# Two transformer blocks on one core: head norms and rotations moved into a projection, a shorter lag behind the gates, gates ahead of the residuals' roots, and a new order in S5

## The chip, the core and the metric

The kernel runs on one core of one Trainium2 chip, as one program with five instruction streams: PE (matmuls), DVE, ACT, POOL and SP, which here issues the DMAs. The metric is the device time of one execution in microseconds (us), median over runs.

## What is computed

512 tokens (256 of context, 256 latent) of width 1024 go through two blocks of two layers each, in float32. The parts that the change touches:

```python
def _rms(x, gain, eps=1e-6):
    xf = x.astype(jnp.float32)
    y = xf * lax.rsqrt(jnp.mean(xf * xf, axis=-1, keepdims=True) + eps)
    return (y * gain.astype(jnp.float32)).astype(x.dtype)
...
    gq, gk, gv, gog, gz, aq, ak, av = _split(h @ w_in, EVEN_SIZES)
    for d, z in enumerate(jnp.split(gz, 2, axis=-1)):
        logit = (z @ gla_w_gate[d] + gla_b_gate[d]).astype(jnp.float32)
        g = _heads(jax.nn.log_sigmoid(logit) / GLA_GATE_TAU, GLA_HEADS)
        dirs.append(_directional_scan(q, k, v, g, n_ctx, reverse=(d == 1)))
...
    qa = _rms(aq.reshape(B, N, ATT_KV_HEADS, ATT_GROUP, ATT_HEAD_DIM), att_q_norm).transpose(0, 2, 3, 1, 4)
    ka = _rms(ak.reshape(B, N, ATT_KV_HEADS, ATT_HEAD_DIM), att_k_norm).transpose(0, 2, 1, 3)
...
    q_lat = _rope(qa[:, :, :, n_ctx:], cos, sin)
    k_all = jnp.concatenate([ka[:, :, :n_ctx], _rope(ka[:, :, n_ctx:], cos, sin)], axis=2)
...
    x_lat = x_lat + m_lat[2] * _rms(o_lat @ w_out, norm_post_mix[l])
```

The first part is the norm; the next ones stand in the first mixer (a gated linear attention beside a softmax attention over k_all); the last line is the residual after a mixer, and the one after a feed-forward part is like it. `m_lat` and `m_ctx` are modulation vectors, products of the conditioning vector with mod_w. The S5 mixer of the second block is a diagonal complex state-space scan: inputs by `b_bar`, a scan over 128-token chunks, outputs by `c_mat`, for 64 groups and two directions.

## The kernel before

Activations stand feature-major: X and H are 128 partitions x 8 tiles x 512 tokens. A float32 product with a weight is made of three rounded ones: of every operand a rounded copy (ACT, `act_part`) and the rest (DVE, `dve_part`) are formed, in HP or XP for activations, in WP for weights. A weight "piece" is 128x1024; it is loaded by SP into one of four slots, split, and used by 24 matmuls.

Each engine has one hand-written order of instructions. `sig` marks an event, `wait_ge` waits for one, `fence` waits for a whole stage, and `take` and `until` hand out the eight PSUM banks. The stages are a list in `program`: the start (`First`), the first mixer (`Even`), feed-forward 0, the second mixer (`Odd`), feed-forward 1, the third mixer (`Mla`), MLP 0, `S5`, MLP 1.

`Even` has three parts. **The projection** (`Projections`, 50 to 166 us): shifts of h (`act_shift`, `dve_shift`), parts of h, then 20 pieces; pieces 12 to 15 give outputs by tokens (`tokens4_pe`), the last four by features (`four_pe`). Between pieces DVE builds the S5 and rotation tables two steps at a time (`beside`); SP stores them (`tables_sp`) and then fetches the mask msk, the gates' weights gla_gw and the constants cst. **The steps** (`Even.pe`, `act`, `dve`, `pool`; 22 of them, 168 to 379 us): step s works on attention unit s - LAG (16 units: scores, maxima, exponentials, transposes, values), on item s (a norm of 128 rows of heads, `RmsHeads`, and its rotation `Rope`, six of each), on the gates of the linear attention (`gates_*`, four of them), on its diagonal levels (`linear_*`), and on rows of the modulation product (`late_mods`: five groups of four steps, each with the two-slot loads of mod_w that `rows` uses, in slots 0 and 1). **The output projection** (`OutProj`, 379 to 423 us) takes its weights through the same slots; `EARLY` says which pieces and parts ACT and DVE prepare in the last three steps.

`Resid` follows the output projections and the feed-forward parts (even.res, ffn0.res over 512 tokens, odd.res, ffn1.res over 256). ACT squares the eight tiles, DVE adds pairs (`add_up`), PE sums over partitions, ACT forms the root as Ln and Exp, and then DVE does for each tile the multiplication with the root RS and, by halves, the addition into X with the factor CO. In ffn1.res PE also sums the squares of the context for the next mixer (`context_pe`), ahead of its own.

`S5` runs four turns u: PE transposes weights (`turn_pe`), ACT copies them to Wb (`turn_act`), PE forms inputs V (`inputs_pe`), DVE scans them (`scan_dve`), PE forms outputs.

In PE's steps late_mods sets which of the four groups of rows, q0 to q3, are read:

```python
            mods, r, k = self.late_mods(s)
            if mods:
                for q in ((0,), (1, 2), (3,), ())[k]:
```

Of the kernel before, what the change touches and what calls it, by code (L numbers as in the profile page):

```python
# [12 lines left out]
ALU = mybir.AluOpType  # L13
# [533 lines left out]
class Norm:  # L547
# [52 lines left out]
    def act(self, act, meanwhile=None):  # L600
        self.head_act(act, meanwhile)
        self.tail_act(act)

# [12 lines left out]

    def tail_act(self, act):
        p, n0 = self.p, self.n0
        self.mods.wait_co(act, self.j)
        for t in range(1, KT, 2):  # L620
            self.act_shift(act, t)
# [40 lines left out]
    def late_dve(self, dve):  # L662
        for t in range(0, KT, 2):
            self.dve_shift(dve, t)

    def parts_act(self, act):
        for k in range(KT):
            self.act_part(act, k)

# [4 lines left out]

    def parts_dve(self, dve):
        for k in range(KT):
            self.dve_part(dve, k)
# [34 lines left out]
class Resid:  # L712
# [3 lines left out]

    def __init__(self, p, name, down, src, n0, j, mods, sq):
# [3 lines left out]
        self.copied = 0 if down.banks is None and not down.add else None  # L721
        self.context = None

    def pe(self, pe):
        p, n, pe = self.p, T - self.n0, pe.on(self.name)
        banks = self.down.banks
        if banks is None:
            pe.core["free"][self.bank] = (self.name, ("y", 0))
# [7 lines left out]
        for t in range(KT):  # L736
            pe.until(t if banks is None else banks[t // 2], "y" if self.down.add else "yn", t)
        pe.until(self.bank, "lnsum")
        if self.context is not None:
            pe.core["free"][self.bank] = (self.context.stage, ("clnsum",))  # L740

    def act(self, act):
        p, n0, n, act = self.p, self.n0, T - self.n0, act.on(self.name)
        for t in range(KT):
            if self.down.add:
                act.wait_ge("y", t)
                y = self.down.Y[:, t, :]
            else:
                act.wait_ge("sum", self.down.c, t, of=self.src)
                y = self.down.at(t)  # L750
            act.act(self.sq[:, t, 0:n], y, ACT.Square).then_inc(*act.sig("sq", t))
# [4 lines left out]
        act.act(rs, rs, ACT.Exp, scale=-0.5).then_inc(*act.sig("rstd"))  # L756
        if self.context is not None:
# [10 lines left out]

    def dve(self, dve):
        p, n0, n, Y, dve = self.p, self.n0, T - self.n0, self.down.Y, dve.on(self.name)  # L770
        for t in range(KT):
            if self.down.add or t == self.copied:
                ps = dve.wait_ge("sum", self.down.c, t, of=self.src)[:, 0:n]
                if not self.down.add:
                    dve.wait_ge("sq", t)
# [3193 lines left out]
```

## Time and profile before

| | us |
|---|---|
| median of 3 runs | 2569.46 |
| lowest, highest | 2567.4, 2573.09 |
| the profiled execution | 2578.15 |
| its span in the trace | 2576.0 |

The span runs from the first to the last recorded instruction; what the execution takes beyond it is not in the trace. Starts are counted from the start of the span. A line of a timeline groups equal instructions that follow each other, with the time from the first one's start to the last one's end. L169, L200 and the like are lines of the helpers that issue matmuls and vector operations, so instructions are told apart by their tiles: sb_WP and sb_HP are the parts, sb_slot the slots, ps a PSUM bank. `PEclk` is the clock that was granted to PE, as a share of the full one.

### The profile page before, as it was taken

How to read it: one execution, taken by the hardware profiler on the slowest of the kernel's cores; microseconds unless marked ns; L12 is line 12 of the kernel's file. 1: busy time of each engine (PE TensorE's matmuls, PEld its weight loads, DVE VectorE, ACT ScalarE, POOL GpSimd, SP SyncE). 2: the span in 40 equal slices, each digit the busy share in tenths (PEclk: the TensorE clock that was granted, in tenths of full speed). 3: DMA queues.
4: the chain of work that ended last, by engine and by line, in shares of the span. 5: the costliest groups of instructions: out<-in, count | busy, mean ns of one | idle time of the engine just before them, and what ended most of it. 6: DMA issues, size and time to landing. Idle time of an engine off the chain costs nothing.

```text
span 2576.0 us, 35431 instructions
## 1 busy us (share of the span) xinstructions
PE 2343.0 (91%) x14834; PEld 1855.0 (72%) x14834; DVE 1501.4 (58%) x2352; ACT 1055.7 (41%) x1780; POOL 220.1 (9%) x302
## 2 busy tenths in 40 slices
PE   5987888999998988887999898989999999998999
PEld 2853455888875866666999672347878877878999
DVE  5337555656555487776544515555656564986554
ACT  3243444322233445554444425544332233335543
POOL 0001200000000033321000002110200200000110
PEclk8988989999999999999999999999999999999999
DMA  7135552444432455333654123342344424434453
GB/s 270 66 143 226 190 203 84 139 143 150 155 115 82 131 164 164 131 131 102 197 172 166 66 85 131 131 164 84 139 147 153 147 106 181 171 118 164 164 189 123
DMA packets 175279, 372.79 MB, mean 145 GB/s; under 512 B 8432, under 2 KB 101872, under 8 KB 160784
## 3 DMA queue, kind: packets, MB, share of 16 engines
q1 hardware_dynamic: 175120, 370.53, 41.0%
q8 instruction: 117, 1.92, 0.3%
q14 instruction: 42, 0.34, 0.0%
HBM read 340.07 MB, written 30.44 MB: 144 GB/s over the span
## 4 chain that ended last, share of the span: by engine, by line
PE 72%; DVE 13%; ACT 7%; issue 4%; DMA 3%; POOL 1%; SPq 0%; DVEq 0%; ACTq 0%; POOLq 0%
PE ps L169 71%; DVE sb_R L200 4%; ACT sb_R L252 2%; DVE sb_X L217 1%; DVE sb_WP L200 1%; DVE sb_H L200 1%; DMA sb_R<-mod_w 1%; DMA sb_slot<-mod_w 1%; DVE sb_cst L214 1%; ACT sb_R L258 1%; PE ps L179 1%; ACT sb_H L252 1%; DVE sb_cst L200 1%; DVE sb_R L232 1%; DVE sb_R L229 1%
## 5 line engine op out<-in xcount | busy, mean ns | idle before, releaser
L169 PE MATMUL ps<-sb_HP,sb_WP 128*128 128x512 f32 (+1 forms) x5736 | 1087.2, 350 | 39.7 <-DVE sb_HP L200 19.7
L169 PEld LDWEIGHTS ps<-sb_HP,sb_WP 128*128 128x128 f32 x5736 | 922.4, 192 | 188.0 <-DVE sb_HP L200 26.2
L200 DVE TENSOR_TENSOR sb_WP<-sb_slot,sb_WP 128x1024 fp32r<-128x1024 f32 x380 | 469.1, 1239 | 613.2 <-ACT sb_WP L258 612.8
L258 ACT ACTIVATE sb_WP<-sb_slot 128x1024 fp32r<-128x1024 f32 x380 | 399.1, 1056 | 745.6 <-PE ps L169 735.0
L169 PE MATMUL ps<-sb_XP,sb_WP 128*128 128x256 f32 (+1 forms) x2976 | 505.1, 333 | 15.3 <-DVE sb_XP L200 15.3
L169 PEld LDWEIGHTS ps<-sb_XP,sb_WP 128*128 128x128 f32 x2976 | 451.4, 193 | 69.0 <-DVE sb_XP L200 17.2
L200 POOL TENSOR_TENSOR sb_R<-sb_R 128x128 f32<-128x128 f32 (+2 forms) x194 | 155.3, 824 | 1581.7 <-ACT sb_R L252 1290.7
L200 DVE TENSOR_TENSOR sb_R<-sb_R 128x256 f32<-128x256 f32 (+3 forms) x398 | 201.1, 539 | 32.2 <-ACT sb_R L252 29.2
L169 PE MATMUL ps<-sb_R 128*32 128x64 f32 (+7 forms) x1768 | 162.6, 290 | 52.9 <-DVE sb_R L200 24.1
L169 PEld LDWEIGHTS ps<-sb_R 128*32 128x32 f32 (+4 forms) x1768 | 115.1, 155 | 109.0 <-issue 66.6
L252 ACT ACTIVATE sb_R<-ps 128x512 f32<-128x512 f32 (+1 forms) x208 | 99.7, 513 | 96.0 <-PE ps L169 92.5
L252 ACT ACTIVATE sb_R<-sb_R 128x512 f32<-128x512 f32 (+4 forms) x128 | 83.7, 663 | 121.5 <-DVE sb_R L200 119.9
L258 ACT ACTIVATE sb_R<-ps 128x512 f32<-128x512 f32 (+5 forms) x163 | 69.7, 495 | 109.5 <-PE ps L169 99.2
L169 PE MATMUL ps<-sb_H,sb_cst 128*128 128x256 f32 (+2 forms) x200 | 79.0, 542 | 33.1 <-ACT sb_H L252 29.2
L169 PE MATMUL ps<-sb_WP,sb_HP 128*128 128x512 f32 (+1 forms) x480 | 101.4, 371 | 4.5 <-DVE sb_HP L200 4.5
L169 PEld LDWEIGHTS ps<-sb_WP,sb_HP 128*128 128x128 f32 x480 | 85.5, 192 | 21.5 <-DVE sb_HP L200 5.3
L169 PEld LDWEIGHTS ps<-sb_H,sb_cst 128*128 128x128 f32 x200 | 37.8, 213 | 70.9 <-issue 29.5
L169 PE MATMUL ps<-sb_slot,sb_SX 128*2 128x512 f32 x544 | 72.6, 640 | 8.1 <-DMA sb_slot<-mod_w 8.1
L258 ACT ACTIVATE sb_slot<-ps 128x256 f32<-128x256 f32 (+3 forms) x124 | 45.5, 402 | 70.0 <-PE ps L179 43.3
L200 DVE TENSOR_TENSOR sb_cst<-sb_cst,sb_R 128x512 f32<-128x512 f32 (+1 forms) x112 | 72.2, 685 | 2.9 <-ACT sb_cst L252 2.5
L200 DVE TENSOR_TENSOR sb_XP<-sb_R,sb_XP 128x256 fp32r<-128x256 f32 (+1 forms) x116 | 64.8, 569 | 14.4 <-ACT sb_XP L258 13.9
L200 DVE TENSOR_TENSOR sb_R<-sb_slot,sb_R 128x2048 f32<-128x2048 f32 (+1 forms) x32 | 54.5, 1755 | 26.4 <-ACT sb_R L258 26.0
(142 smaller groups left out, 1822.8 us busy)
## 6 DMA issues: line engine op xcount, KB each, us to landing
sb_slot<-mlp_w SPq DMA_DIRECT2D x32, 2048.0 KB, 8.9
sb_slot<-mod_w SPq DMA_DIRECT2D x22, 2048.0 KB, 8.8
sb_R<-ada_w SPq DMA_DIRECT2D x12, 2048.0 KB, 7.4
sb_slot<-ada_w SPq DMA_DIRECT2D x24, 1024.0 KB, 4.8
sb_slot<-ffn_w_gate SPq DMA_DIRECT2D x22, 1024.0 KB, 5.3
sb_slot<-ffn_w_up SPq DMA_DIRECT2D x22, 1024.0 KB, 7.8
sb_slot<-ffn_w_down SPq DMA_DIRECT2D x10, 2048.0 KB, 7.7
sb_slot<-odd_w_in SPq DMA_DIRECT2D x32, 512.0 KB, 7.2
```

What stands on the lines that cost most here:

```text
L169: return self.e.matmul(out, w, x, start=start, stop=stop, skip_group_check=True)
L179: return self.e.transpose(out, a, self.p.c("ident"))
L200: return BLANK if self.e is None else self.e.tensor_tensor(out, a, b, op)
L214: return self.e.tensor_scalar(out, a, s1, None, op0) if op1 is None else self.e.tensor_scalar(out, a, s1, s2, op0, op1)
L217: return BLANK if self.e is None else self.e.scalar_tensor_tensor(out=out, in0=a, scalar=s, in1=b, op0=op0, op1=op1)
L229: return BLANK if self.e is None else self.e.reduce_max(out, a, AX.X)
L232: return BLANK if self.e is None else self.e.tensor_tensor_scan(out, a, b, 0.0, ALU.mult, op)
L252: return self.e.activation(out, a, func, bias=bias, scale=scale)
L258: return self.e.activation(out, a, ACT.Copy) if scale is None else self.e.activation(out, a, ACT.Copy, scale=scale)
```

## The change

It has six parts.

- Start of the projection: shifts, parts and the first three pieces are interleaved tile by tile (`FIRST`), where all shifts, then all parts, then the pieces stood.
- SP: two projection loads, then gla_gw and cst, then the rest of the projection; msk stays behind the tables.
- Items: norms and rotations are issued between projection pieces 12 to 19 (`ITEMS`, `between`), with banks 3 to 6 for the first ones; DVE's last rotation follows the projection.
- Steps: LAG is 2 for 4, so 20 steps. `late_mods` starts at step 0 for step 1, one step later relative to the units.
- `Resid`: the factor CO is multiplied before the root (`gate_act`, `gate_dve`; PSUM is free after it), blocks are two plain operations, tiles 2 and 5 on POOL. ffn1.res sums the context after its own sum.
- `S5`: turns go through i first and take banks 4 to 7 in the first turn; inputs wait for each half's Wb and each h; the scan starts after the first half of the inputs.

```diff
 class Resid:
+    POOL = (2, 5)
...
+        self.late = 6 if n0 == 0 else 8
...
         pe.vacant(self.bank)
-        if self.context is not None:
-            self.context.context_pe(pe, p.ps[self.bank])
         for g, group in enumerate(self.groups):
...
         pe.until(self.bank, "lnsum")
         if self.context is not None:
+            pe.vacant(self.bank)
+            self.context.context_pe(pe, p.ps[self.bank])
...
+    def gate_act(self, act, t):
...
+            i = act.copy(Y[:, t, a:b], y[:, a:b], self.mods.CO[:, self.j, w, t:t + 1])
+        i.then_inc(*act.sig("gated", t))
...
+    def block(self, e, t):
...
+        e.wait_ge("rstd")
+        e.wait_ge("gated", t)
+        e.mul(Y[:, t, :], Y[:, t, :], p.RS[:, n0:T]).then_inc(*e.sig("yn", t))
+        e.wait_ge("yn", t)
+        e.add(p.X[:, t, n0:T], p.X[:, t, n0:T], Y[:, t, :]).then_inc(*e.sig("x", t))
...
         for t in range(KT):
-            dve.mul(Y[:, t, :], y, p.RS[:, n0:T]).then_inc(*dve.sig("yn", t))
-            dve.wait_ge("yn", t)
-            for w, a, b in halves(n0):
-                i = dve.stt(p.X[:, t, a:b], Y[:, t, a - n0:b - n0], self.mods.CO[:, self.j, w, t:t + 1], p.X[:, t, a:b], ALU.mult, ALU.add)
+            if t not in self.POOL:
+                self.block(dve, t)
+    def pool(self, pool):
+        for t in self.POOL:
+            self.block(pool.on(self.name), t)
...
 class Projections:
+    FIRST = (0, 2, 4)
...
+            self.norm.dve_shift(e, 0)
+            self.norm.dve_shift(e, 2)
+            for t in range(KT):
+                if t in self.FIRST:
+                    self.pieces.dve_part(e, self.FIRST.index(t))
+                self.norm.dve_part(e, t)
+                if t % 2 == 0 and t + 4 < KT:
+                    self.norm.dve_shift(e, t + 4)
...
         for x in self.pieces.dve_ahead(e):
             next(beside, None)
             next(beside, None)
+            if between is not None:
+                between(x)
...
 class Even:
-    LAG = 4
+    LAG = 2
+    ITEMS = {12: (0, None), 13: (1, 0), 14: (2, 1), 16: (3, 2), 17: (4, 3), 18: (5, 4), 19: (None, 5)}
...
-        self.proj.sp(sp)
+        self.proj.first_sp(sp)
         e.fence(*self.before)
+        e.dma(self.gw[0:32], p.io["gla_gw"]).then_inc(*e.full("full_gw", "gw"))
+        e.dma(p.cst[:, 256:NEARLY], p.io["cst"][:, 256:NEARLY]).then_inc(*e.full("full_cst", "consts"))
+        self.proj.sp(sp, 2)
         self.params.tables_sp(sp)
-        e.dma(self.m, p.io["msk"]).then_inc(*e.full("full_late", "late_m"))
+        e.dma(self.m, p.io["msk"]).then_inc(*e.full("full_late", "late"))
...
-        r, k = divmod(s - 1, 4)
+        r, k = divmod(s, 4)
...
-    FIRST, VALUES = (4, 13), (12, 19)
+    FIRST, VALUES = (LAG, LAG + 9), (LAG + 8, LAG + 15)
     EARLY = ((0, 1), (0, 1)), ((2,), (2, 3)), ((), (4,))
...
 class S5:
-        for s in range(4):
-            if s == 3:
-                e.wait_ge("W3", u)
-            for i in range(2):
-                b, ps = e.take(0, 4)
+        for i in range(2):
+            for s in range(4):
+                if s == 3:
+                    e.wait_ge("W3", u)
+                b, ps = e.take(*(0, 4) if u else (4, 8))
...
-        e.wait_ge("Wb", u, 3, 1)
-        for k in range(KT):
-            e.wait_ge("h", k, of="s5.in")
         for i in range(2):
+            e.wait_ge("Wb", u, 3, i)
...
+                e.wait_ge("h", 4 * fh + f, of="s5.in")
...
-        e.wait_ge("V", u, 3, 1)
+        e.wait_ge("V", u, 3, 0)
...
         e.mul(T1, pr, Vr).then_inc(*e.sig())
+        e.mul(Vr, pi, Vr).then_inc(*e.sig())
+        e.wait_ge("V", u, 3, 1)
         e.mul(T2, pi, Vi).then_inc(*e.sig())
-        e.mul(Vr, pi, Vr).then_inc(*e.sig())
```

The first place in the order is PE at the end of the first mixer's projection, before. sb_WP,sb_HP are projection matmuls (pieces by tokens, then by features), `sb_R 128x512 x4` the gates' logits, `sb_cst 128x512` the sums of an item's norm, `sb_R,sb_cst 128x256` a rotation, `sb_slot0,sb_SX` rows of a modulation group from slot 0:

```order
L169 MATMUL ps<-sb_WP,sb_HP 128x512 x96
L169 MATMUL ps<-sb_HP,sb_WP 128x512 x96
L169 MATMUL ps<-sb_R 128x512 x4
L169 MATMUL ps<-sb_cst 128x512 x2
L169 MATMUL ps<-sb_R,sb_cst 128x256
L169 MATMUL ps<-sb_slot0,sb_SX 2x512 x8
L169 MATMUL ps<-sb_cst 128x512
L169 MATMUL ps<-sb_R,sb_cst 128x256
L169 MATMUL ps<-sb_slot1,sb_SX 2x512 x8
L169 MATMUL ps<-sb_slot0,sb_SX 2x512 x8
L169 MATMUL ps<-sb_cst 128x512
```

And now, from the first piece by features on:

```order
L169 MATMUL ps<-sb_HP,sb_WP 128x512 x24
L169 MATMUL ps<-sb_cst 128x512
L169 MATMUL ps<-sb_R,sb_cst 128x256
L169 MATMUL ps<-sb_HP,sb_WP 128x512 x24
L169 MATMUL ps<-sb_cst 128x512
L169 MATMUL ps<-sb_R,sb_cst 128x256
L169 MATMUL ps<-sb_HP,sb_WP 128x512 x24
L169 MATMUL ps<-sb_cst 128x512
L169 MATMUL ps<-sb_R,sb_cst 128x256
L169 MATMUL ps<-sb_HP,sb_WP 128x512 x24
L169 MATMUL ps<-sb_R,sb_cst 128x256
L169 MATMUL ps<-sb_R 128x512 x4
```

The items now stand between pieces of 24 matmuls, and the rows of the modulation follow the logits directly, with the first unit's scores (`sb_R 128x256 x2`) behind the third group of rows.

The second place is PE's last steps ahead of the output projection (`x192`), before. sb_slot2,sb_R are products of the linear attention, sb_cst,sb_slot3 transposes and sb_slot3,sb_R values of the attention:

```order
L169 MATMUL ps<-sb_slot2,sb_R 128x256 x2
L169 MATMUL ps<-sb_slot1,sb_SX 2x512 x8
L169 MATMUL ps<-sb_R,sb_cst 128x512 x2
L179 MATMUL ps<-sb_cst,sb_slot3 128x128 x4
L169 MATMUL ps<-sb_slot3,sb_R 64x128 x8
L179 MATMUL ps<-sb_cst,sb_slot3 128x128 x4
L169 MATMUL ps<-sb_cst,sb_RW 128x128 x4
L169 MATMUL ps<-sb_slot3,sb_R 64x128 x8
L169 MATMUL ps<-sb_HP,sb_WP 128x512 x192
```

And now:

```order
L169 MATMUL ps<-sb_slot2,sb_R 128x256 x2
L169 MATMUL ps<-sb_slot1,sb_SX 2x512 x8
L169 MATMUL ps<-sb_slot0,sb_SX 2x512 x8
L169 MATMUL ps<-sb_R,sb_cst 128x512 x2
L179 MATMUL ps<-sb_cst,sb_slot3 128x128 x4
L169 MATMUL ps<-sb_slot3,sb_R 64x128 x8
L179 MATMUL ps<-sb_cst,sb_slot3 128x128 x4
L169 MATMUL ps<-sb_slot1,sb_SX 2x512 x8
L169 MATMUL ps<-sb_slot3,sb_R 64x128 x8
L169 MATMUL ps<-sb_cst,sb_RW 128x128 x4
L169 MATMUL ps<-sb_HP,sb_WP 128x512 x192
```

Rows from slots 1 and 0 (q1, q2) now stand in the last unit's step, behind the linear attention, and the fourth rows behind the values of the next step; before, the fourth rows from slot 1 were the only ones there.

## Rows read from the trace of the kernel before

**Rows 1.** page, part 1: busy us, share of the span, instructions
```profile
PE 2343.0 (91%) x14834; PEld 1855.0 (72%) x14834; DVE 1501.4 (58%) x2352; ACT 1055.7 (41%) x1780; POOL 220.1 (9%) x302
```

**Rows 2.** page, part 4: shares of the chain that ended last
```profile
PE 72%; DVE 13%; ACT 7%; issue 4%; DMA 3%; POOL 1%; SPq 0%; DVEq 0%; ACTq 0%; POOLq 0%
```

**Rows 3.** windows: stretch, us, busy (instructions) by engine, PEclk, DMA share, GB/s
```profile
50.05:166.26 116.21, 116.21 (x552) 95.81 (x552) 43.46 (x114) 29.59 (x40) 0.00 (x0) 0.98 0.25 82
201.55:359.12 157.57, 121.09 (x951) 70.91 (x947) 105.33 (x188) 67.30 (x169) 30.27 (x18) 0.89 0.50 194
359.12:378.90 19.78, 17.46 (x109) 9.64 (x105) 6.35 (x8) 10.39 (x20) 0.00 (x0) 0.91 0.71 276
```

**Rows 4.** timeline 38 to 60, DVE and PE: start us, us, what, [idle before <-releaser]
```profile
48.69 4.62 DVE L200 TENSOR_TENSOR sb_WP<-sb_slot,sb_WP 128x1024 fp32r<-128x1024 f32 x4
...
50.05 20.17 PE L169 MATMUL ps<-sb_HP,sb_WP 128*128 128x512 f32 x80 [11.83 <-DVE sb_WP L200]
```

**Rows 5.** DMA issues from 21.8 to 22.1: KB each, median us to landing
```profile
sb_slot<-even_w_in SPq DMA_DIRECT2D x1, 2048.0 KB, 17.4
```

**Rows 6.** timeline, PE, 148 to 206
```profile
202.86 1.12 PE L169 MATMUL ps<-sb_cst 128*128 128x512 f32 x2 [0.60 <-ACT sb_cst L252]
```

**Rows 7.** timelines of DVE, SP and PE, 153 to 168; DMA issues at 158.9 and 160.2
```profile
153.53 0.06 DVE L223 MEMSET sb_RS<- 128x1 f32 x1
166.40 0.63 DVE L220 CAST sb_msk<-sb_R 128x896 uint8<-128x896 f32 x1 [12.81 <-DMA sb_cst<-cst]
...
158.98 0.33 SPq L263 DMA_DIRECT2D sb_R<-msk  x1
...
167.71 5.05 PE L169 MATMUL ps<-sb_R 32*128 32x512 f32 x8 [1.45 <-ACT sb_R L252]
...
sb_R<-msk SPq DMA_DIRECT2D x1, 448.0 KB, 2.9
...
sb_slot<-mod_w SPq DMA_DIRECT2D x1, 2048.0 KB, 11.0
```

**Rows 8.** timeline, PE: rows of two mod_w loads
```profile
193.59 3.49 PE L169 MATMUL ps<-sb_slot,sb_SX 128*2 128x512 f32 x16 [3.68 <-DMA sb_slot<-mod_w]
...
357.29 1.90 PE L169 MATMUL ps<-sb_slot,sb_SX 128*2 128x512 f32 x16 [0.35 <-DMA sb_slot<-mod_w]
```

**Rows 9.** DMA issues at 357.0 and 360.6; timeline, ACT, 346 to 382
```profile
sb_slot<-mod_w SPq DMA_DIRECT2D x1, 2048.0 KB, 7.3
...
sb_slot<-even_w_out SPq DMA_DIRECT2D x1, 512.0 KB, 8.8
...
372.27 2.00 ACT L258 ACTIVATE sb_WP<-sb_slot 128x1024 fp32r<-128x1024 f32 x2
```

**Rows 10.** timelines of DVE and POOL: a residual's block, POOL beside DVE
```profile
437.54 0.68 DVE L200 TENSOR_TENSOR sb_R<-ps,sb_RS 128x512 f32<-128x512 f32 x1
438.26 0.88 DVE L217 SCALAR_TENSOR_TENSOR sb_X<-sb_R,sb_CO,sb_X 128x256 f32<-128x256 f32 x2
...
207.95 2.96 DVE L200 TENSOR_TENSOR sb_R<-sb_R 128x512 f32<-128x512 f32 x3 [0.33 <-ACT sb_R L252]
...
208.09 1.67 POOL L200 TENSOR_TENSOR sb_R<-sb_R 128x512 f32<-128x512 f32 x1 [207.65 <-ACT sb_R L252]
211.05 2.51 POOL L200 TENSOR_TENSOR sb_R<-sb_R 128x512 f32<-128x512 f32 x2 [1.29 <-ACT sb_R L252]
```

**Rows 11.** timeline, PE, 1407 to 1428
```profile
1412.03 3.62 PE L169 MATMUL ps<-sb_H,sb_cst 128*128 128x256 f32 x16
```

**Rows 12.** timelines of PE and DVE in S5
```profile
2168.83 11.57 PE L169 MATMUL ps<-sb_H,sb_R 32*128 32x128 f32 x197 [2.49 <-ACT sb_H L252]
...
2289.74 6.69 DVE L200 TENSOR_TENSOR sb_R<-sb_slot,sb_R 128x2048 f32<-128x2048 f32 x3 [6.43 <-ACT sb_R L258]
...
2320.73 0.88 PE L169 MATMUL ps<-sb_R,sb_slot 128*32 128x64 f32 x48 [0.66 <-DVE sb_R L200]
```

More of the change, by code:

```diff
@@ L746, in act @@
                 act.wait_ge("y", t)
[L747 removed]
             else:
                 act.wait_ge("sum", self.down.c, t, of=self.src)
[L750 to L751 removed]
+            act.act(self.sq[:, t, 0:n], self.src_of(t), ACT.Square).then_inc(*act.sig("sq", t))
+        for t in range(4, self.late):
+            self.gate_act(act, t)
         act.wait_ge("sumsq")
@@ L756, in act @@
         act.act(rs, rs, ACT.Exp, scale=-0.5).then_inc(*act.sig("rstd"))
+        for t in range(self.late, KT):
+            self.gate_act(act, t)
         if self.context is not None:
@@ L891, in out_loads, with four_pe @@
     return [load(order[0:4]), load(order[4:8])]
-def four_pe(p, pe, pieces, x, n, u, cols):
+def four_pe(p, pe, pieces, x, n, u, cols, between=None):
     bs = []
@@ L942, in tokens4_pe @@
                 pe.E.at[pe.stage, "used", y] = pe.E.at[pe.stage, "out", u, 3]
+            if between is not None:
+                between(y)
 def narrow_pe(p, pe, pieces, u, blocks):
@@ L1324, in sp, with first_sp, pe @@
         self.pieces.sp(sp.on(self.name), None, first)
-    def pe(self, e):
+    def first_sp(self, sp):
+        for n in range(2):
+            self.pieces.load(sp.on(self.name), n)
+    def pe(self, e, between=None):
         p = self.p
@@ L1332, in pe @@
             if kind == "tokens":
-                tokens4_pe(p, e, pieces, u)
+                tokens4_pe(p, e, pieces, u, between)
             elif kind == "narrow":
@@ L1348, in act @@
             for _ in range(4):
-                next(ahead)
+                y = next(ahead)
+                if between is not None:
+                    between(y)
             for a, out in enumerate(outs):
@@ L1358, in act, with dve @@
                 i.then_inc(*e.sig("taken", u, a))
-    def dve(self, e, beside=()):
+    def dve(self, e, beside=(), between=None):
         if self.early:
-            self.norm.late_dve(e)
-            self.norm.parts_dve(e)
-            self.pieces.dve_first(e)
+            self.norm.dve_shift(e, 0)
+            self.norm.dve_shift(e, 2)
+            for t in range(KT):
+                if t in self.FIRST:
+                    self.pieces.dve_part(e, self.FIRST.index(t))
+                self.norm.dve_part(e, t)
+                if t % 2 == 0 and t + 4 < KT:
+                    self.norm.dve_shift(e, t + 4)
         else:
@@ L1370, in dve @@
             next(beside, None)
+            if between is not None:
+                between(x)
         for _ in beside:
```

150 lines of the change are left out of this document (81 added, 69 removed).

## Prediction

> **What bounds the kernel now.** I read the page first. PE is busy 91% of the span, DVE 58%, ACT 41% and POOL 9% [rows 1], and the chain that ended last runs 72% on PE, 13% on DVE, 7% on ACT and 3% on DMA [rows 2]. So an instruction costs what it weighs only where PE has no gap; elsewhere, moved work can be free. Then I cut the span at the stages and read busy time in each [rows 3]. The projection of the first mixer (50.05 to 166.26) has PE busy in all of its 116.21 us: work put there is paid in full. In the mixer's steps up to the last unit's scores (201.55 to 359.12) PE is busy for 121.09 of 157.57 us, at a clock of 0.89: these steps hang on hand-offs between engines and on the loads of mod_w as well as on PE. From the last scores to the output projection there are 19.78 us. Last I read single instructions at the places that the change touches.
>
> **Start of the projection.** DVE ends a piece by subtracting its rounded part, the first four from 48.69 on, and PE, which has stood idle for 11.83 us, begins at 50.05 [rows 4]. It needs only the first piece. The first load, issued at 21.89, lands 17.4 us later [rows 5], at 39.3. Now ACT copies piece 0 first (2.00 for two in rows 9, so 1.1 with its start, to 40.4), DVE subtracts it (4.62 / 4 = 1.16, to 41.6), then the first part, half as wide (0.6), so PE begins near 42.35: **-7.7**. Afterwards PE takes 5.5 us for a piece of 24 matmuls and the two other engines need about 2.7 for a part and a piece, so they stay ahead.
>
> **Norms and rotations in the projection.** Six matmuls of 128x512 and six of 128x256 come onto PE's full stretch. One matmul with float32 operands runs as two in the trace; a pair of the first kind took 1.12 with 0.60 of idle before it [rows 6], and the second is half as wide, 0.56. In a full stretch a wide matmul takes 116.21 / 552 = 0.21 for one split in three; at twice that for each half of a float32 one, 0.86 for a pair and 0.43 for a narrow pair, I get 6 x 0.86 + 6 x 0.43 = 7.7 at least, and 6 x 1.12 + 6 x 0.56 = 10.1 at most: **+8**, nearest to the row of full stretches, since the matmuls of the next piece fill what a pair would wait for. DVE and ACT are busy for 43.46 and 29.59 us of the 116.21 [rows 3], so their share of the items hides there. Sum of the two parts: the last projection matmul ends at about 166.7 instead of 166.3.
>
> **The mask arrives late.** DVE builds the rotation tables between pieces, 45 steps at two for a piece; the last five now stand behind the norm of item 5. They ended at 153.53 [rows 7]; I place them at 165.7. SP stores them, waits for the store, and issues msk 5.4 us after their end (158.98), which lands 2.9 later, and the cast of 0.63 follows. Before, that chain ended in cst (166.40), and PE's first logits began at 167.71. After: 165.7 + 5.4 + 2.9 + 0.64 = 174.6, and PE goes on at 175.0. The work that used to hide the mask is the projection itself; it no longer does. **+7.3** as a wait. The gates' weights and the constants, which SP now fetches before the projection's remaining loads, cost nothing: the projection moves 25% of what the DMA engines could [rows 3].
>
> **To the first scores.** The mod_w loads go out behind msk, at 171.4 instead of 160.30, and the third needs a slot that the first one's rows free. Before, PE read the third load's rows at 193.59 after waiting 3.68 us for it, and the first scores followed at 201.55 [rows 3, 8]. The first landed in 11.0 [rows 7]. After: rows of load one at 182 to 184, a load of 7.3 [rows 9] to 191.5, two us of rows, so scores at 193.4. With two steps fewer between the gates and the first unit this is **-8.2** against 201.55, everything above included.
>
> **The steps.** From first to last scores it was 157.57 us. Items are gone from units 0 to 3, but the gates of the second pair of heads now stand beside units 0 and 1, where they formerly ran ahead. I count **-2.5** (0 to -5 as bounds). The last unit's scores then start at 348.4.
>
> **The tail.** The output projection needs w_out in a slot, copied and subtracted. Before, the slot that its first load takes was free one step earlier: the last of that load's four parts was issued at 360.6 and took 8.8, and ACT copied at 372.27 [rows 9]. The first of the four was issued 1.3 earlier, so all have landed 10.1 after it. The mod_w schedule (late_mods) now stands one step later relative to the units, so rows q1 and q2 of the last group are read in the last unit's own step, as the second place in the order shows. They are read 12 to 16 us after its scores (an estimate: transposes, copies and values of two units stand before them in the order); then the load goes out and takes 10.1 for its parts; the two piece copies (2.00 in rows 9), their subtractions, the roots and the last turns take 11. That is 37 us from last scores to output projection, where 19.78 were needed: **+17**. Row 0 of the output projection would start at 385.4 instead of 378.90. A PE that has stood idle begins at less than its full clock (0.91 in the stretch before [rows 3]), about +0.8. Sum of all up to here: **+7.3**.
>
> **The four residuals.** In the two wide ones a block was 0.68 and 0.88 on DVE [rows 10], 1.515 with the overlap, eight of them 12.1. After: six blocks of two plain tensor operations, 1.33 each, 8.0. POOL takes blocks 2 and 5: four operations. POOL's 128x512 operation ran 1.67 beside DVE's three, which took 2.96 instead of 3 x 0.64 = 1.9 [rows 10]: about 1.0 lost to DVE for each. 8.0 + 4 x 1.0 = 12.0, and 12.7 if the ends don't meet: **+0.3** each. The gates before the root fit in the time in which PE sums squares. The odd residual, half as wide, likewise +0.3. In the last one (ffn1.res) 16 matmuls of the next mixer's context stood before the sums of squares, 3.62 us [rows 11]; they go behind the root. DVE's adds and ACT's squares bound it next, about 1.5 earlier only, and POOL gives back some of that: I take **-2.0**. Sum **-1.1**; bounds -4 (POOL free of cost) and +2. The Trainium skill (SBUF — State Buffer, section "SBUF: two separate sides") says that a GpSimd operation and a VectorE operation with two SBUF inputs exclude each other for the whole instruction. By that rule the 12 DVE operations and four POOL ones of a wide residual would follow each other, 12 x 0.68 + 4 x 1.26 = 13.2 with POOL's operation at 2.51 for two [rows 10], 1.1 more than now, and the four would sum to about +2.
>
> **S5.** PE's inputs began at 2168.83 after 2.49 us for the last shifted h; they now need the first of them only, and PE takes a second four banks for its turns, so that it starts these straight after its sum, ahead of a root step of about 0.9: together 3.4. Scan 3 starts its three multiplications (6.69) at 2289.74; two of them can now start ahead of the last input, worth up to 4.5, but PE waited only 0.66 for the scan's result at 2320.73 [rows 12], so little of that is seen before PE's own chain is earlier. So **-4.5**: 3.4 + 0.7 and about 0.4 between the two halves of the inputs; bounds -2 and -8.5.
>
> **Sum**: 7.3 - 1.1 - 4.5 = +1.7. On the profiled execution, 2578.15, this gives 2579.9. The median of the runs shown, 2569.46, is 8.7 below that execution; on it, 2571.2. I forecast **2571**. A difference under 0.2%, 5 us, is not told from none.
>
> **Rivals.** *The tail costs nothing* (0.30). w_out's slot may come free in time, or the units run closer together than before, since PE has 36 us idle in the 157.57 [rows 3]. For it: the wait in the tail is built from places in the order, not seen. Against: SP takes its loads strictly in turn. If the 17 us shrink to between 3 and 10, the time is 2557 to 2564: faster; I take 2561. *The mod_w loads fall behind at each group* (0.20). Loads go through slots that PE's rows free, and one takes 7.3 to 11.0 us [rows 7, 9] where a step takes about ten. With PE's rows one step later in the order and the units starting eight us earlier, two or three groups may each wait the 3.7 seen in rows 8: +9, that is 2580, slower. It decides from a step shorter than a load's landing. For it: the wait of rows 8 is there already. Against: the last group waited 0.35 [rows 8]. *POOL and DVE exclude each other* (0.08): the sum of the residuals is +2 instead of -1.1, the time 2574. For it: 2.96 for three operations that take 1.9. Against: only 1.0 was lost beside an operation of POOL that takes 1.26 alone. The Trainium skill's page SBUF — State Buffer is behind this one. My own case, with a wait for the mask and one for w_out, has 0.42, and its range by itself is 2565 to 2576.
>
> **Numbers.** The forecast is 2571. Faster by over 0.2% (under 2564.3): nearly all of the first rival and 0.02 of mine, 0.31. Slower (over 2574.6): the second rival, 0.03 of the third, 0.04 of mine, 0.27. The same: 0.42. The range leaves out the lowest and the highest tenth, which lie in the first two rivals: 2557 to 2582.
>
> **What would show it.** PE should begin the projection near 42.4 and the logits near 175; an idle time before the logits whose releaser is the cast of the mask is the third step. First scores near 193, last near 348, and a gap of PE before the output projection of over 10 us that ends with sb_WP or a load of w_out. In the residuals, DVE's operations longer than 0.69 beside POOL. In ffn1.res the root 2 to 3 us earlier. In S5 PE's inputs near 2166 in the old count. I am wrong if the output projection starts before 375 (tail), if the logits start at once after the projection (mask), or if the residuals change by more than 1 us each.

## The result

The changed kernel took 2589.11 us, median of 4 runs (2587.65 to 2590.69); the one before 2570.79 (2567.4 to 2573.09). The ratio is 1.0068, with a 95% interval of 1.0052 to 1.0084: some 18 us slower, outside the range of 2557 to 2582. The profiled execution of the changed kernel took 2590.69, its span is 2588.9.

The page of the changed kernel, parts 1 and 4, answers to [rows 1] and [rows 2]:

```profile
PE 2346.1 (91%) x14834; PEld 1863.1 (72%) x14834; DVE 1509.1 (58%) x2342; ACT 1063.9 (41%) x1804; POOL 240.4 (9%) x318
...
PE 74%; DVE 11%; ACT 7%; issue 4%; DMA 2%; POOL 1%; SPq 0%; DVEq 0%; ACTq 0%; POOLq 0%
```

PE's busy time rose by 3.1 us, the span by 12.9. So most of the loss is idle time of PE, and the page does not show where. The windows by stage do (the stretches of [rows 3], and between them the one from the projection to the first scores; the columns are the same):

```profile
41.23:172.95 131.72, 127.61 (x576) 102.51 (x576) 58.86 (x146) 48.81 (x73) 0.00 (x0) 0.95 0.17 55
172.95:202.87 29.92, 16.78 (x58) 3.90 (x57) 7.56 (x10) 9.98 (x15) 0.00 (x0) 0.61 0.83 333
202.87:358.17 155.30, 117.90 (x924) 69.75 (x920) 101.73 (x178) 64.99 (x165) 29.22 (x18) 0.87 0.49 191
358.17:396.54 38.37, 23.99 (x141) 11.70 (x137) 8.80 (x12) 14.68 (x26) 0.00 (x0) 0.78 0.48 181
```

The projection takes 131.72 us for 116.21, the steps 155.30 for 157.57, and the way from the last scores to the output projection 38.37 for 19.78. The granted clock fell where PE waits: 0.61 between projection and first scores, 0.78 in the tail. A share of 0.50 is the lower of the two levels, 1.2 GHz; the logits, behind PE's longest wait there, ran at 0.50 throughout (181.18 to 188.34). By landmarks, the change stands as follows on the kernel before (us, PE):

| landmark | before | forecast | after |
|---|---|---|---|
| projection starts | 50.05 | 42.35 | 41.23 |
| its last matmul ends | 166.3 | 166.7 | 172.9 |
| logits start | 167.71 | 175.0 | 181.18 |
| first scores | 201.55 | 193.4 | 202.87 |
| last unit's scores | 359.12 | 348.4 | 358.17 |
| output projection starts | 378.90 | 385.4 | 396.54 |
| next matmul behind even.res | 445.48 | | 464.31 |

PE's timeline of the changed kernel at the first four, against [rows 4], [rows 7] and [rows 8]:

```profile
41.23 48.41 PE L169 MATMUL ps<-sb_HP,sb_WP 128*128 128x512 f32 x201 [6.13 <-DVE sb_HP L200]
...
144.14 8.04 PE L169 MATMUL ps<-sb_HP,sb_WP 128*128 128x512 f32 x24 [4.11 <-DVE sb_cst L200]
...
181.18 7.16 PE L169 MATMUL ps<-sb_R 32*128 32x512 f32 x8 [8.23 <-DVE sb_msk L220]
...
199.34 3.60 PE L169 MATMUL ps<-sb_slot,sb_SX 128*2 128x512 f32 x16 [4.91 <-DMA sb_slot<-mod_w]
```

The start came as forecast. The wait of 4.11 us ahead of the piece at 144.14 was not in the forecast, and that piece took 8.04 us instead of 5.84, at a granted clock of 0.69 where the next piece had 1.00. DVE's timeline tells what released it:

```profile
141.64 1.23 DVE L200 TENSOR_TENSOR sb_WP<-sb_slot,sb_WP 128x1024 fp32r<-128x1024 f32 x1 [5.50 <-ACT sb_WP L258]
...
143.58 0.42 DVE L200 TENSOR_TENSOR sb_cst<-ps,sb_cst 128x256 f32<-128x256 f32 x1
```

The first matmuls of the pieces by features need a PSUM bank that holds item 1's rotated product. DVE reads it at 143.58, in the callback of piece 16, and that stands behind the subtraction of the next piece (141.64), which waits until ACT has copied the outputs by tokens. The bank is free 0.42 later, and PE goes on at 144.14. That this is the cause is a reading of the trace so far; e1_bank below tests it.

SP and the mask, against [rows 7]:

```profile
171.69 0.34 SPq L263 DMA_DIRECT2D s_tabc<-sb_R  x1
...
176.91 0.33 SPq L263 DMA_DIRECT2D sb_R<-msk  x1
177.29 195.28 SPq L263 DMA_DIRECT2D sb_slot<-mod_w  x20
```

The tables end at 171.67, behind the norm of item 5 as forecast, though 6 us later. msk goes out 5.2 later, is cast at 180.35, and the logits start at 181.18. In the tail, ACT, SP and PE, against [rows 9] and the second order:

```profile
358.31 14.26 SPq L263 DMA_DIRECT2D sb_slot<-mod_w  x2
373.92 21.41 SPq L263 DMA_DIRECT2D sb_slot<-even_w_out  x8
```

```profile
385.30 2.00 ACT L258 ACTIVATE sb_WP<-sb_slot 128x1024 fp32r<-128x1024 f32 x2 [13.86 <-DMA sb_slot<-even_w_out]
387.21 1.13 ACT L258 ACTIVATE sb_HP<-sb_H 128x512 fp32r<-128x512 f32 x2
388.25 0.57 ACT L258 ACTIVATE sb_slot<-ps 128x512 f32<-128x512 f32 x1
```

```profile
370.25 3.62 PE L169 MATMUL ps<-sb_slot,sb_SX 128*2 128x512 f32 x32
...
388.88 1.11 PE L179 MATMUL ps<-sb_cst,sb_slot 128*128 128x128 f32 x4 [11.64 <-ACT sb_slot L258]
...
396.54 3.70 PE L169 MATMUL ps<-sb_HP,sb_WP 128*128 128x512 f32 x15
```

SP issues the first part of w_out at 373.92, when PE has read the rows of slot 0 (the 32 matmuls from 370.25). ACT copies it at 385.30, and behind this copy stands the one that the last transposes wait for (388.25), so PE waits 11.64 us ahead of 388.88. That is the tail that the prediction priced at 37 us; it took 38.4.

A wide residual, even.res: DVE, POOL and PE, against [rows 10]:

```profile
444.44 0.69 DVE L200 TENSOR_TENSOR sb_R<-sb_R,sb_RS 128x512 f32<-128x512 f32 x1 [0.31 <-ACT sb_RS L252]
445.17 1.64 DVE L200 TENSOR_TENSOR sb_X<-sb_X,sb_R 128x512 f32<-128x512 f32 x1
446.73 1.75 DVE L200 TENSOR_TENSOR sb_R<-sb_R,sb_RS 128x512 f32<-128x512 f32 x1
448.51 1.64 DVE L200 TENSOR_TENSOR sb_X<-sb_X,sb_R 128x512 f32<-128x512 f32 x1
...
451.86 0.69 DVE L200 TENSOR_TENSOR sb_X<-sb_X,sb_R 128x512 f32<-128x512 f32 x1
```

```profile
444.49 1.77 POOL L200 TENSOR_TENSOR sb_R<-sb_R,sb_RS 128x512 f32<-128x512 f32 x1 [98.03 <-ACT sb_RS L252]
446.33 1.59 POOL L200 TENSOR_TENSOR sb_X<-sb_X,sb_R 128x512 f32<-128x512 f32 x1
447.89 1.71 POOL L200 TENSOR_TENSOR sb_R<-sb_R,sb_RS 128x512 f32<-128x512 f32 x1
449.68 1.60 POOL L200 TENSOR_TENSOR sb_X<-sb_X,sb_R 128x512 f32<-128x512 f32 x1
```

```profile
441.07 1.96 PE L169 MATMUL ps<-sb_H,sb_cst 128*128 128x512 f32 x4 [0.71 <-DVE sb_H L200]
447.61 2.05 PE L169 MATMUL ps<-sb_H,sb_cst 128*128 128x512 f32 x2 [4.59 <-ACT sb_H L252]
450.87 8.95 PE L169 MATMUL ps<-sb_H,sb_cst 128*128 128x512 f32 x14 [1.21 <-ACT sb_H L252]
464.31 6.05 PE L169 MATMUL ps<-sb_HP,sb_WP 128*128 128x512 f32 x14 [4.50 <-DVE sb_HP L200]
```

Beside POOL a DVE operation takes 1.64 to 1.75, alone 0.69. All six blocks take 12.1 us, as the eight did before. From PE's first sums to the next stage's first matmul it is 23.24 us instead of 21.98. PE sums the squares in the order of the tiles. Three of the four slowed operations stand in DVE's order ahead of the end of tile 1, at 450.15, and PE can go on with that tile only at 450.87; POOL's tile 2 had been ready since 447.92. From there the squares come bunched, and PE runs 14 matmuls from 450.87 to 459.82, 0.64 each, where it once kept up with tiles that came 1.52 apart. In ffn1.res PE now sums first:

```profile
1435.69 1.10 PE L169 MATMUL ps<-sb_R,sb_cst 128*128 128x256 f32 x4 [1.02 <-DVE sb_R L200]
1437.36 3.72 PE L169 MATMUL ps<-sb_H,sb_cst 128*128 128x256 f32 x16 [0.56 <-ACT sb_RS L252]
1442.49 3.69 PE L169 MATMUL ps<-sb_H,sb_cst 128*128 128x256 f32 x16 [1.41 <-ACT sb_H L252]
1450.26 6.28 PE L169 MATMUL ps<-sb_HP,sb_WP 128*128 128x512 f32 x14 [4.08 <-DVE sb_HP L200]
```

From the last projection matmul (1434.7) to the next stage's first (1450.26) it is 15.6 us; before it was 17.9, from 1412.2 to 1430.08, with the context's 3.62 us [rows 11] ahead of the sums. In S5, against [rows 12], the inputs start without a wait, straight behind the turns, and the scan begins with two multiplications ahead of the third:

```profile
2183.79 14.98 PE L169 MATMUL ps<-sb_H,sb_R 32*128 32x128 f32 x256
```

```profile
2298.16 4.49 DVE L200 TENSOR_TENSOR sb_R<-sb_slot,sb_R 128x2048 f32<-128x2048 f32 x2 [3.98 <-ACT sb_R L258]
2305.62 2.29 DVE L200 TENSOR_TENSOR sb_R<-sb_slot,sb_R 128x2048 f32<-128x2048 f32 x1 [2.97 <-ACT sb_R L258]
```

From the first sum ahead of S5 to the first matmul of MLP 1 it is 171.3 us (2171.73 to 2343.01) instead of 176.8 (2153.09 to 2329.90).

### The profile page after: what moved, and what is told of

Its sections match the earlier page's. It is cut to its first block, busy times and chain, and to the rows that moved or that the text cites. A ratio compares the mean times of both kernels' runs of the same rounds, so it can differ in the third digit from the quotient of the medians.

```text
span 2588.9 us, 35481 instructions
## 1 busy us (share of the span) xinstructions
PE 2346.1 (91%) x14834; PEld 1863.1 (72%) x14834; DVE 1509.1 (58%) x2342; ACT 1063.9 (41%) x1804; POOL 240.4 (9%) x318
## 4 chain that ended last, share of the span: by engine, by line
PE 74%; DVE 11%; ACT 7%; issue 4%; DMA 2%; POOL 1%; SPq 0%; DVEq 0%; ACTq 0%; POOLq 0%
PE ps L169 74%; DVE sb_R L200 3%; ACT sb_R L252 2%; DVE sb_WP L200 1%; DVE sb_H L200 1%; DMA sb_slot<-mod_w 1%; DVE sb_cst L214 1%; PE ps L179 1%; ACT sb_R L258 1%; DVE sb_cst L200 1%; ACT L245 1%; DMA sb_slot<-even_w_in 1%; DVE sb_X L217 1%; DVE sb_R L229 1%; ACT sb_H L252 1%
## 5 line engine op out<-in xcount | busy, mean ns | idle before, releaser
L169 PE MATMUL ps<-sb_R 128*32 128x64 f32 (+7 forms) x1768 | 166.3, 295 | 60.3 <-DVE sb_R L200 23.4
L169 PEld LDWEIGHTS ps<-sb_WP,sb_HP 128*128 128x128 f32 x480 | 85.5, 192 | 22.1 <-DVE sb_HP L200 5.3
L169 PE MATMUL ps<-sb_slot,sb_SX 128*2 128x512 f32 x544 | 76.2, 674 | 10.7 <-DMA sb_slot<-mod_w 10.7
```

Of the source, the lines that this page charges most:

```text
L169: return self.e.matmul(out, w, x, start=start, stop=stop, skip_group_check=True)
```

## The experiments

All ratios are to the kernel before, with 95% intervals; the changed kernel's is 1.0068. One thousandth is 2.6 us.

**The three waits, one by one.**

```diff
# e1_bank: items_dve
+        if y == 15:
+            self.rope_dve(dve, 1)
         if n1 is not None:
             dve.wait_ge("consts", of="even.in")
-            if n1:
+            if n1 not in (0, 2):
                 self.rope_dve(dve, n1 - 1)
```

> The changed kernel, but DVE's rotation of item 1 stands at projection piece 15 instead of 16, ahead of the preparation of the next piece. Theory A (PE's gap of 4.11 us ahead of the first piece by features is a wait for the PSUM bank that this rotation reads): the gap goes, and with it the slow clock behind it (8.04 instead of 5.84 us for that piece), 6.3 us in all; the tables, the mask, the logits and the first scores come 6 us earlier, and the time is near 2583. Rival B (the first scores are set by the mod_w loads, which do not care): the projection ends 6 us earlier and the first scores come at most 1 us earlier; the time stays near 2589.

Measured: 1.0052 (1.0037 to 1.0067), 4 us less than the change. PE at the first piece by features:

```profile
142.90 3.74 PE L169 MATMUL ps<-sb_HP,sb_WP 128*128 128x512 f32 x15 [0.69 <-ACT sb_cst L252]
```

The gap shrank from 4.11 to 0.69 us and the logits came at 175.23 instead of 181.18, the whole 6 us, and first scores at 197.06 for 202.87; the output projection started at 392.33, 4.2 earlier. The bank was the cause, and the loads did not hide it.

```diff
# e2_tables: Projections.dve
-            next(beside, None)
-            next(beside, None)
+            for _ in range(3):
+                next(beside, None)
```

> The changed kernel, but DVE makes three table steps per projection piece instead of two, so that they end at piece 15 instead of behind the last norm. Theory A: the mask is there before the projection ends; PE's wait of 8.23 us ahead of the logits goes, the logits run at the full clock, and the mod_w loads, which stand behind the mask on SP, go out as soon as their slots are free, so that the waits of 4.91 and 1.58 us for them shrink too. First scores 12 to 17 us earlier, time near 2575. Rival B (loads cannot start before the projection's last slots are free, about when the mask passes now): only 2 to 4 us.

Measured: 1.0027 (1.0013 to 1.004). PE at the end of the projection:

```profile
143.72 5.72 PE L169 MATMUL ps<-sb_HP,sb_WP 128*128 128x512 f32 x24 [3.32 <-DVE sb_cst L200]
...
172.28 6.82 PE L169 MATMUL ps<-sb_R 32*128 32x512 f32 x8 [2.07 <-DVE sb_R L200]
...
190.41 3.21 PE L169 MATMUL ps<-sb_slot,sb_SX 128*2 128x512 f32 x16 [5.89 <-DMA sb_slot<-mod_w]
```

The logits wait 2.07 us for DVE's last rotation and no longer 8.23 for the mask, and start 8.9 us earlier; the output projection started 13.5 earlier. But the logits kept the lower clock (6.82), and the third mod_w load was still awaited for 5.89, though the first two were issued from 143 on: its slot comes free only when PE reads the first rows. The first scores gained 9.3, not the 12 to 17 expected, so rival B was half right.

```diff
# e3_phase: late_mods and the groups of rows in PE's steps
-        r, k = divmod(s, 4)
+        r, k = divmod(s + 1, 4)
...
-                for q in ((0,), (1, 2), (3,), ())[k]:
+                for q in ((0,), (0, 1, 2) if s == 0 else (1, 2), (3,), ())[k]:
...
-        self.more.cols_dve(dve, 2)
```

> The changed kernel, but each modulation step is one step earlier relative to the attention units, as before the change: the first step reads three groups of rows, and the last group's third rows are read in the step before the last unit's. Theory A (the slot of w_out's first load comes free too late): PE's way from the last unit's scores to the output projection falls from 38.4 to about 20 us; the first scores may come up to 6 us later, since the fourth rows stand before them; time 2572 to 2578. Rival B (ACT's and DVE's preparation of w_out simply moved behind other work): the tail keeps over 30 us, time 2589 or more.

Measured: 1.0026 (1.0015 to 1.0036). The tail fell to 19.77 us:

```profile
369.30 1.13 PE L169 MATMUL ps<-sb_R 64*128 64x512 f32 x4
...
389.07 3.24 PE L169 MATMUL ps<-sb_HP,sb_WP 128*128 128x512 f32 x13
```

The first scores came 4.3 us later and the steps took 162.1 us, so in the profiled execution (2586.62 us, 5 above the median of its runs) the output projection started only 7.5 earlier; the ratio gives 11. The cause of the tail is shown: w_out's slot, through the place of the third rows. e4_three has all three edits.

> The changed kernel with all three edits of this batch: rotation 1 read earlier, three table steps per piece, modulation one step earlier. Theory A: the gains add up, 6 + 14 + 14, and the time is near 2555, faster than the kernel before by 0.6%. Rival B (one wait stands behind the other): the sum is no better than the best of the three alone by more than 5 us, so 2568 or more.

Measured: 0.9992 (0.9981 to 1.0003), 19 us less than the change, near to the sum of the single gains (4 + 11 + 11 = 26 at most) but with some of it hidden. So the three waits together cost about as much as the change lost. Yet 2555 was not reached, although start and S5 should gain some 13 us (7.7 and 5.4): theory A's sum fell short, and where these gains went is taken up with e13 below.

**The residuals and S5.** e5_resid_only and e6_s5_only put one class of the change's diff into the kernel before, `Resid` with its calls on POOL, and `S5`.

> The kernel before with only the residuals of the change (gates ahead of the root, plain blocks, tiles 2 and 5 on POOL, the context behind the root in ffn1.res). Prediction: the four residuals together -1.1 us, 2570 on the old median. Theory C (the squares come in another order and bunched, so that PE's sums behind them run late and slowly): the three others 1 to 1.5 us longer each from the root to the next matmul, ffn1.res 1 to 2 shorter; +2 in all. Rival D (DVE and POOL exclude each other for the whole time): wide residuals +1.2 in DVE's own blocks already.

> The kernel before with only the new order in S5. Predicted -4.5 us; in the changed kernel the stage took 4.5 less. Theory: it is worth the same alone, since nothing in it hangs on the other parts: ratio 0.998. Rival: part of it was the loads and the state of the clock that the stage was entered with, and alone it gives under 2 us.

Measured: the residuals 1.0014 (1.0003 to 1.0024), so 3.6 us slower; S5 0.9979 (0.9968 to 0.9991), 5.4 faster. From PE's sums to the next stage even.res took 23.20 instead of 21.98, the odd one 14.68 instead of 13.56, and ffn1.res 2.3 less. e7_three_oldresid gives e4_three its old residuals back.

> The kernel of e4_three with the residuals of the kernel before. Theory C: 2 us faster than e4_three, ratio to the kernel before near 0.998. Rival (the new residuals are worth -1.1 as predicted): 1 us slower, ratio 1.000.

Measured: 0.9972 (0.9957 to 0.9987), 5 us faster than e4_three; even.res took 21.98 again. e9_nopool_only keeps the change's residuals and takes only POOL out of them, on the kernel before:

```diff
-    POOL = (2, 5)
+    POOL = ()
```

> The residuals of the change alone on the kernel before (as in e5_resid_only), but with all blocks on DVE, none on POOL. Theory G (gates ahead of the root and plain blocks gain 8 x 0.18 us in a wide residual; it is POOL that gives it back, through DVE's operations of 1.64 to 1.75 beside it and PE's sums, which are bunched at the end): a wide residual is 1.3 us shorter than before and 2.5 shorter than with POOL, ffn1.res 2.3 shorter; ratio 0.998. Rival H (PE's sums bound the residual either way, 16 matmuls of 0.64): no better than 1.001.

Measured: 0.9988 (0.9978 to 0.9997), 3.1 us faster than before and 6.7 faster than with POOL (e5). even.res took 20.44 us. ffn1.res was only 0.6 us shorter than before in this trace (17.3 for 17.9), not the 2.3 expected: its 16 context matmuls took 5.41 us at a granted clock of 0.68, and 3.72 at 1.00 in e5. The same residual in e10_best_nopool, DVE's first block and PE:

```profile
413.40 0.69 DVE L200 TENSOR_TENSOR sb_R<-sb_R,sb_RS 128x512 f32<-128x512 f32 x1 [0.31 <-ACT sb_RS L252]
414.12 0.69 DVE L200 TENSOR_TENSOR sb_X<-sb_X,sb_R 128x512 f32<-128x512 f32 x1
```

```profile
410.02 1.95 PE L169 MATMUL ps<-sb_H,sb_cst 128*128 128x512 f32 x4 [0.72 <-DVE sb_H L200]
415.63 10.34 PE L169 MATMUL ps<-sb_H,sb_cst 128*128 128x512 f32 x16 [3.65 <-ACT sb_H L252]
430.47 5.02 PE L169 MATMUL ps<-sb_HP,sb_WP 128*128 128x512 f32 x11 [4.50 <-DVE sb_HP L200]
```

Every operation takes 0.69, eight blocks 10.7 us instead of the 12.1 of six beside POOL, and PE ends its sums at 425.97, 1.8 us after DVE's last addition. So the gates ahead of the root, with the plain blocks, were worth 1.5 us in a wide residual (21.98 to 20.45), and POOL gave back 2.8 (23.24 to 20.45): it took four operations of 0.69 off DVE and made four others 1.0 longer, three of them ahead of the end of tile 1. Rival H fell.

**What is behind the mask.** e8_rowsfirst is e4_three with PE reading the first two groups of rows ahead of the logits:

```diff
         self.proj.pe(e, lambda y: self.items_pe(a, y))
+        for q in (0, 1):
+            self.mods.rows_pe(pe, 1, q)
         pe.fence("even.in")
...
-                for q in ((0,), (0, 1, 2) if s == 0 else (1, 2), (3,), ())[k]:
+                for q in ((0,), (2,) if s == 0 else (1, 2), (3,), ())[k]:
```

> The kernel of e4_three, but PE reads the first two groups of modulation rows straight after the projection, ahead of the gates' logits. Theory E (the first scores hang on the third and fourth mod_w loads, which can only be issued when the first two have been read, and those land long before): the first scores come 6 to 9 us earlier, ratio near 0.996. Rival F (the steps behind are bound by the chain of gates, maxima and exponentials from the logits on): the first scores come earlier, the last ones not, ratio unchanged at 0.999.

Measured: 0.9939 (0.9915 to 0.9962), 14 us less than e4_three in ratio. The output projection started only 7.3 earlier, but the profiled execution of e8_rowsfirst, 2562.45 us, was the longest of its four, and the two kernels were timed in different batches; so the gain lies somewhere near 7 to 14 us. PE:

```profile
178.19 3.42 PE L169 MATMUL ps<-sb_slot,sb_SX 128*2 128x512 f32 x16 [2.33 <-DMA sb_slot<-mod_w]
184.43 3.36 PE L169 MATMUL ps<-sb_slot,sb_SX 128*2 128x512 f32 x16 [2.82 <-DMA sb_slot<-mod_w]
187.72 0.89 PE L169 MATMUL ps<-sb_R 64*128 64x256 f32 x4
```

The wait for the third load is down from 5.67 us (e4_three) to 2.33, that for the fourth is 2.82 as before (2.74); the first scores come at 187.72, 10.4 us earlier, and the logits took 3.70 at the full clock. Theory E holds, with more than it forecast. The last scores came 5.6 earlier.

e10_best_nopool and e11_best_oldresid are e8_rowsfirst with the residuals of e9 and with the old ones; e12_lag4 has the lag of 4 again:

```diff
# e12_lag4, on e8_rowsfirst
-    LAG = 2
+    LAG = 4
...
-        r, k = divmod(s + 1, 4)
+        r, k = divmod(s - 1, 4)
...
-                for q in ((0,), (2,) if s == 0 else (1, 2), (3,), ())[k]:
+                for q in (() if s == 1 else (0,), (2,) if s == 2 else (1, 2), (3,), ())[k]:
```

> The kernel of e8_rowsfirst with all residual blocks on DVE. Theory G: 5 us faster than e8_rowsfirst, ratio 0.992. Rival H: no difference from e8_rowsfirst, 0.994.

> The kernel of e8_rowsfirst with the residuals of the kernel before. If e7_three_oldresid against e4_three holds here: 3 to 5 us faster than e8_rowsfirst, ratio 0.992 to 0.993, and by theory G 2 to 3 us slower than e10_best_nopool.

> The kernel of e8_rowsfirst with a lag of 4 again, so 22 steps; norms and rotations stay in the projection. Theory I (what the change gains in the steps is the shorter lag: with 4, the units wait for all four gates and the fourth load): the first scores come 6 to 12 us later, the steps behind them are at most 3 us shorter, time 4 to 9 us longer, ratio 0.996 to 0.998. Rival J (the steps are bound by the chains of the linear attention, which start with the gates and not with the units): ratio as e8_rowsfirst, 0.994.

Measured: 0.9928 (0.9913 to 0.9943), 0.9947 (0.993 to 0.9963) and 0.9931 (0.9916 to 0.9947). The order of e10 and e11 is that of theory G, with intervals that overlap. The shorter lag bought nothing: with 4 the first scores came at 186.03, no later than with 2, and the steps took 154.2 us. Theory I fell, and rival J holds for the time. It may even be that the lag of 2 costs something. e12_lag4 still has POOL in its residuals and is level with e10_best_nopool, which has not, and its output projection starts at 360.01, where the three kernels with a lag of 2 (e8, e10, e11) start theirs at 365.34 to 370.02. With POOL at 6.7 us that points to some 5 us for the lag of 4; with four runs of each it is not shown.

**The place of the items.** e13_old_mixer is the changed kernel with the whole `Even` class of the kernel before, so without the diff's lines under `class Even`, and with POOL out of the residuals as in e9; e14_old_mixer_rows adds three table steps per piece and the two groups of rows ahead of the logits.

> The changed kernel with the first mixer of the kernel before (norms and rotations in the steps, lag 4, the old schedule of modulation and of SP), with the change's start of the projection and its S5, and with the residuals on DVE alone. Theory K (moving the norms and rotations costs its 8 us in the projection and gives nothing back, since the steps hang on other chains): the parts add up, -7.7 for the start, -5.4 for S5 and -3 for the residuals, ratio 0.9935 to 0.995. Rival L (the steps without the items are shorter by what the items took): ratio 0.997 or more, since the start alone is lost again in a wait for the constants.

> The kernel of e13_old_mixer with three table steps per piece and with the first two groups of modulation rows ahead of the logits, so that only the place of the norms and rotations and the lag tell it from e10_best_nopool (0.9928). Theory K: the same or faster, 0.989 to 0.993. Rival L: slower than e10_best_nopool by 3 us or more, 0.994 or more.

Measured: 0.9938 (0.9925 to 0.995) and 0.9923 (0.9909 to 0.9936). Start, S5 and residuals add up to 16 us (7.7 + 5.4 + 3.1, where 7.7 is the forecast, since no run has the start alone), as theory K had it. e4_three, which has the items in the projection, is 14 us slower than e13: POOL is 6.7 of it, and its output projection starts 6.7 later (373.88 for 367.16). That is where the gains of e4 went: the move costs 8 to 9 us in the projection, and with the first scores hanging on the third and fourth load about half of it was still there at the first scores (198.12 for 193.87), and 6.7 at the output projection, behind steps of 155.98 us for 153.54. With the rows early, the place of the items makes no difference that the runs can tell (0.9928 and 0.9923): in e14 PE went on behind the projection at 158.38, in e10 at 167.52, and those 9.1 us were spent by the first scores (187.00 and 186.61). The two also differ in the lag; e12_lag4, with the items in the projection and the lag of e14, starts its output projection at 360.01, e14 at 361.13. e14 is the fastest kernel of the study, 2550.96 us, 0.8% under the kernel before; e10 can't be told from it.

## Why the prediction was wrong

- **Start, -7.7.** Right: PE began at 41.21 to 42.84 in all kernels with the change's start, and at 48.95 to 50.32 in the four without it.
- **Norms and rotations, +8.** A little small. The price of a norm and rotation was right: a piece of 24 matmuls with them took 6.78 us (152.02 to 158.80), where one alone took 5.5 before, and 0.86 + 0.43 had been forecast. Without the bank's wait the whole projection took 125.2 us (e1) to 126.3 (e4) for 116.2, so 9 to 10; with the new start and no items it took 117.1 (e13), so 8 to 9 are the items'. "DVE and ACT ... their share of the items hides there" is the step that failed: their busy time did hide, but the order did not. One read of DVE's stood behind a subtraction that waited for ACT and PE, and its bank was the next that PE needed. That put 6.3 us on PE, the wait with the slow piece, and e1_bank shows the cause: moving that one read brought the logits 6.0 us forward. The prediction had no term for such a wait.
- **The mask, +7.3.** The wait was right (8.23 for 8.3), the mechanism too (e2_tables); its place was 6 us late, by the step above.
- **First scores, 193.4.** 9.5 off: 6.2 from the above and 3.3 from rows read at a low clock behind the wait. The two groups of rows took 6.16 us at a granted clock of 0.58, so the slot of the first came free, and the third load was issued, at 191.93, 1.7 later than forecast; and the third group's own rows took 3.60 us where I had two. PE had stood idle for 1.45 us ahead of the logits before and for 8.23 now.
- **The steps, -2.5.** 155.30 for 157.57, as forecast to 0.3, but that is luck: the steps of the kernel before, in three more profiles of kernels that left them unchanged (e5, e6, e9), took 159.9, 151.4 and 154.5.
- **The tail, +17.** Right: 38.4 for the forecast 37 (e3_phase: 19.8 without its cause).
- **The residuals, -1.1.** Wrong in sign, +3.6 (0.8 to 6.2). DVE's own sum held: 4 times 1.0 lost beside POOL, 12.1 us for a forecast of 12.0 to 12.7. I stopped at DVE's last addition. What follows is PE's sum in the order of the tiles, and DVE's slowed tile 1 held it up until seven tiles were left for the end; PE ended 3.3 us behind DVE, 1.8 before. The rule that I had weighed against it (the Trainium skill, SBUF — State Buffer, "SBUF: two separate sides") forbids that a DVE and a POOL operation overlap for any part, 13.2 us for DVE's blocks. The trace has 12.1, but four DVE operations beside POOL's are 1.0 longer each, so it agrees in kind and not in the sum; e9 shows that taking POOL away is worth 2.8 us in each wide residual.
- **S5, -4.5.** Right within its bounds: -5.5 between the traces (not the 4.5 that the expectation of e6 names), 5.4 by the ratio of e6. The inputs came 3.7 earlier, for 3.4; 1.5 lie behind the last scan, 1.0 of it in a gap of PE (4.62 us before, 3.63 now) for which the trace shows no releaser.
- **The sum against the median.** I set +1.7 on the profiled execution and carried it to the median unchanged. On the profiled executions the error is 10.8 us (2590.7 for 2579.9): some 10 in the mixer, which is 17.6 later at the output projection for a forecast of 7.3 (6.2 + 3.3 and 1.6 of steps and tail, less the 0.8 that I had put in for the clock), and about 1 behind it. The other 7 us are the step from the profiled execution to the median. That of the kernel before was 7.4 us above the median, that of the changed kernel 1.6, so the medians differ by 18.3 where the profiles differ by 12.5. The likely place is the mixer's steps: the same mixer started its output projection at 378.90, 379.20, 370.31 and 373.55 in four profiles. That it was so in this execution is not shown, since the other runs have no trace.

The rival of mod_w loads that fall behind at each group, which had the slower side with 2580, did not happen: PE's waits for mod_w between 41 and 400 us came to 10.7 us in four waits, 8.1 in six before. The rival without a tail did not either. My own case was the right one, with two waits as named; a third wait, a slower clock behind it, the residuals' end and the step from the profiled execution to the median put it beyond its range.

## What to carry to other kernels

When work is moved between the instructions of a full stretch, sum its time, but then follow each buffer that it holds (here a PSUM bank) to the instruction that frees it, and ask what that one stands behind on its own engine. A load that waits for a slot should be traced back to the read that frees the slot, and that read put as early as its data allows: reading two groups of rows ahead of the logits, and the last ones a step earlier, were worth some 7 to 14 us and 11 us here, each about as much as the moved work cost. The shorter lag, which looks like a gain on paper, bought nothing here. And take several profiles of a kernel before a term of a few us is read from one, above all where steps hang on loads.

## What the runs showed that I had not expected

The same instructions of the mixer's steps took 151.4, 154.5, 157.6 and 159.9 us in four profiles (e6, e9, before, e5), and went with the granted clock: 0.95, 0.94, 0.89 and 0.88. The fastest, e6_s5_only:

```profile
200.82:352.22 151.40, 112.24 (x950) 65.55 (x946) 105.60 (x188) 67.25 (x169) 30.28 (x18) 0.95 0.53 202
352.22:370.31 18.09, 15.77 (x108) 9.05 (x104) 6.35 (x8) 10.38 (x20) 0.00 (x0) 1.00 0.82 316
```

Its clock was 1.00 in the tail, 0.91 in the kernel before [rows 3]; in the steps PE was busy for 112.24 us instead of 121.09 with the same instructions. What decides between them, and whether the clock is cause or effect of the waits, is not shown. The other point: POOL costs DVE about 1.0 us for each operation that they share, whether the DVE operation writes X or the scratch tile, and in these wide residuals, where DVE is the bound up to tile 1, that made the helper a loss of 2.8 us.
